# A hybrid two-layer encoder block on one core: conditioning loads and products moved ahead, a head's normalisation moved ahead of a weight split, four banks claimed at once

## The reference, cut to what matters

```
c_act = silu(c)
mod = c_act @ cond_w[layer] + cond_b[layer]          # (1, 6*1024): 12 pieces of 512 columns a layer
# layer 0: f = gated DeltaNet (4 heads, chunks of 64) beside window attention (8 heads), then SwiGLU
a_qkv, a_z, a_a, a_b, b_q, b_k, b_v = split_cols(h @ w_in, EVEN_WIDTHS)
# layer 1: f = retention, then top-2-of-8 expert SwiGLU
q, k, v, g = split_cols(h @ w_in, ODD_WIDTHS)        # 4 heads: q, k 256 wide, v, g 512 wide
y = multiscale_retention(rotary(q), rotary(k), v)    # per head
y = (y - mean(y)) * rsqrt(var(y) + eps) * gn_w       # the head's normalisation
out = (silu(g) * y) @ w_out
```

## Time and profile before

| | |
|---|---|
| median of 3 runs | 1683.41 us (1683.18 to 1684.49) |
| the profiled execution, its own time | 1683.41 us |
| its span in the profile | 1681.5 us |
| TensorE busy | 1602.5 us, 95% |
| VectorE busy | 1289.4 us, 77% |
| ScalarE busy | 1010.4 us, 60% |
| DMA, mean | 306 GB/s |

### The profile page before, as it was taken

The page is one execution under the profiler, slowest core; times in us unless marked ns, Lnnn a source line. Parts: engine busy times, 40 slices in busy tenths (PEclk is TensorE's granted clock), DMA queues, the critical chain, the costliest instruction groups (busy, mean ns, idle before and its releaser), DMA issues.

```text
span 1681.5 us, 20080 instructions
## 1 busy us (share of the span) xinstructions
PE 1602.5 (95%) x7810; PEld 1289.5 (77%) x7810; DVE 1289.4 (77%) x1176; ACT 1010.4 (60%) x868; POOL 104.3 (6%) x78
## 2 busy tenths in 40 slices
PE   3899999999989999699999999999999999999996
PEld 1785766888868888578888888888888888888875
DVE  1675657655577665889898898898898988988987
ACT  0452335444354553377777777777777777777775
POOL 0003110200001002010000000000000000000004
PEclk9999999999999999799999999999999999999998
DMA  9579596954545544499999999999999999999994
GB/s 327 198 279 336 209 366 213 299 188 167 211 135 175 191 152 139 164 350 396 376 388 377 377 389 372 385 389 369 384 389 370 388 383 373 389 385 362 389 377 151
DMA packets 234370, 515.33 MB, mean 306 GB/s; under 512 B 8936, under 2 KB 40960, under 8 KB 234176
## 3 DMA queue, kind: packets, MB, share of 16 engines
q1 hardware_dynamic: 228272, 491.99, 79.9%
q10 hardware_dynamic: 2992, 11.79, 2.0%
q0 software_dynamic: 3008, 10.20, 2.0%
HBM read 507.15 MB, written 13.11 MB: 309 GB/s over the span
## 4 chain that ended last, share of the span: by engine, by line
PE 91%; DVE 4%; DMA 2%; ACT 1%; issue 1%; POOL 0%; POOLq 0%; SPq 0%; DVEq 0%
PE bank L752 27%; PE bank L754 27%; PE bank L753 27%; PE bank L731 2%; PE bank L923 2%; DMA ring<-in_cond_w 2%; PE bank L1189 1%; PE bank L747 1%; PE bank L1101 1%; PE bank L1171 0%; DVE w_lo L1679 0%; PE bank L764 0%; PE bank L1180 0%; PE bank L984 0%; PE bank L1132 0%
## 5 line engine op out<-in xcount | busy, mean ns | idle before, releaser
L1679 DVE TENSOR_TENSOR w_lo<-ring,w_hi 128x2048 fp32r<-128x2048 f32 x336 | 764.7, 2290 | 104.3 <-ACT w_hi L1564 102.3
L1564 ACT ACTIVATE w_hi<-ring 128x2048 fp32r<-128x2048 f32 x334 | 640.5, 1918 | 195.2 <-PE bank L754 190.3
L752 PE MATMUL bank<-w_lo,heT_hi 128*128 128x512 f32 x896 | 353.9, 395 | 3.8 <-DVE w_lo L1679 2.2
L754 PE MATMUL bank<-w_hi,heT_hi 128*128 128x512 f32 x896 | 349.9, 391 | 0.0
L753 PE MATMUL bank<-w_hi,heT_lo 128*128 128x512 f32 x896 | 349.1, 390 | 0.0
L1668 DVE TENSOR_TENSOR w_part<-ring,w_part 128x1024 fp32r<-128x1024 f32 (+1 forms) x162 | 201.1, 1250 | 164.1 <-ACT w_part L1316 158.7
L1316 ACT ACTIVATE w_part<-ring 128x1024 fp32r<-128x1024 f32 (+1 forms) x162 | 169.2, 1049 | 234.1 <-PE bank L754 219.5
L752 PEld LDWEIGHTS bank<-w_lo,heT_hi 128*128 128x128 f32 x896 | 168.4, 188 | 39.0 <-issue 5.9
L754 PEld LDWEIGHTS bank<-w_hi,heT_hi 128*128 128x128 f32 x896 | 168.2, 188 | 35.7
L753 PEld LDWEIGHTS bank<-w_hi,heT_lo 128*128 128x128 f32 x896 | 168.5, 188 | 33.5
L752 PE MATMUL bank<-w_part,hT_hi 128*128 128x512 f32 (+1 forms) x448 | 178.8, 399 | 6.1 <-DVE hT_lo L1659 5.0
(11 more groups left out here) (345 smaller groups left out, 1532.4 us busy)
## 6 DMA issues: line engine op xcount, KB each, us to landing
ring<-in_moe_w_up SPq DMA_DIRECT2D x224, 1024.0 KB, 8.6
ring<-in_moe_w_down SPq DMA_DIRECT2D x112, 1024.0 KB, 7.3
ring<-in_cond_w SPq DMA_DIRECT2D x24, 2048.0 KB, 10.0
ring<-in_ffn_w_up SPq DMA_DIRECT2D x22, 1024.0 KB, 8.2
ring<-in_od_w_in SPq DMA_DIRECT2D x8, 2048.0 KB, 7.9
ring<-in_ev_w_in SPq DMA_DIRECT2D x5, 2048.0 KB, 10.1
ring<-in_ffn_w_down SPq DMA_DIRECT2D x5, 2048.0 KB, 7.5
ring<-in_od_w_in SPq DMA_DIRECT2D x8, 1024.0 KB, 7.7
```

The costliest lines, as they stand in the source:

```text
L752: mm(bank, lhs[0], rhs[1], start=start, stop=False)
L754: return mm(bank, lhs[0], rhs[0], start=False, stop=stop)
L1564: f(w_hi[:, n % 3], half_landed(act, it, u, half), ACT.Copy) \
L1679: tt(w_lo[:, buf], at, w_hi[:, buf].bitcast(F32), ALU.subtract).then_inc(S["w_lo"], 1)
```

## The change

Four edits in one.

The loads: a conditioning unit is put in front of `ev_in` 5, 4 and 3 each (two in front of 3), so that unit 5, 4 and 3 stand one, one and two places later than before (and from `cond(0, 10)` on the order is as it was). `COND_BATCHES` moves two units from its third batch to its second.

The rows: `cond_rows()` also runs after `ev_in` 2, and after `ev_in` 4 it takes two instead of one; after chunk 2 of the recurrence none is taken, and the last call takes one instead of two.

The banks: `down` claims its four banks ahead of its first part instead of each when it is first used.

The head's normalisation: ScalarE and VectorE no longer split part 3 of `od_v` ahead of `deviations` and `head_norm(h-1)`; the following `split_ahead("od_v", h)` does it after them.

```diff
-COND_BATCHES = (tuple((0, u) for u in FIRST_COND), tuple((0, u) for u in range(4, N_COND)) + tuple((1, u) for u in range(3)),
-                tuple((1, u) for u in range(3, N_COND)))
+COND_BATCHES = (tuple((0, u) for u in FIRST_COND), tuple((0, u) for u in range(4, N_COND)) + tuple((1, u) for u in range(5)),
+                tuple((1, u) for u in range(5, N_COND)))
...
-    order = c(0, *FIRST_COND) + e(0) + c(0, 4) + e(1) + c(0, 5) + e(2, 5) + c(0, 6) + e(4)
-    order += c(0, 7) + e(3) + c(0, 8, 9, 10, 11) + c(1, *range(N_COND))
+    order = c(0, *FIRST_COND) + e(0) + c(0, 4) + e(1) + c(0, 5) + e(2) + c(0, 6) + e(5) + c(0, 7)
+    order += e(4) + c(0, 8, 9) + e(3) + c(0, 10, 11) + c(1, *range(N_COND))
...
-                if u < 2:
-                    cond_rows()
+                cond_rows()
...
             project(("ev_in", 5), 0, 256)
             cond_rows()
             project(("ev_in", 4), 0, second=norms, second_at=(2, 0))
-            cond_rows()
+            cond_rows(2)
             project(("ev_in", 3), 0, second=norm_rows, second_at=(2, 0))
             cond_rows(2)
...
-                if n < 3:
+                if n < 2:
                     cond_rows()
...
-                outs = {}
+                outs = {(t, h): to_fill(pe, kind, t, h) for t in range(NT) for h in range(2)}
...
-                            if ch == 0:
-                                outs[t, h] = to_fill(pe, kind, t, h)
...
                 if h:
-                    split_to(part_no["od_v", h, 3] + 1)
                     deviations("ret_var", "ret_rstd", NT * (h - 1), eps_n)
                 split_ahead("od_v", h)
...
                 if h:
-                    split_to(part_no["od_v", h, 3] + 1)
                     head_norm(h - 1)
                 split_ahead("od_v", h)
```

## The result

The changed kernel takes 1699.40 us (median of 4 runs, 1696.13 to 1700.53) where the kernel before took 1683.73 us beside it (4 runs, 1683.18 to 1684.49). The ratio is 1.0101, with a 95% interval of 1.0086 to 1.0117: slower, by 15.7 us between the medians. The forecast was 1697.0. The profiled execution took 1700.71 us, 17.3 more than the one of before.

A forecast was written before the change was run, and what follows sets the result against it. TensorE, busy 95% of a 1681.5 us span, was taken as the bound. Terms 3.7 + 2.8 - 0.6 + 6.6 + 1.1 = 13.6 us on 1683.4 gave 1697.0 us, with an 8 in 10 range of 1690.5 to 1702.

The forecast's parts named there:

- term 2: At the first matmul of ev_in 4, TensorE waits 2.8 us because the unit's load lands late; ends 0 and 4.
- Term 1: Ahead of g_row, two more conditioning rows at 1.85 us each make it 3.7 us later; a cost of 3.7 us.
- prediction's own sign of being wrong: Wrong if g_row came within 2 us of its old time, od_v showed no wait, or the clock fell in new places.
- the rival's four falls: Each of four new TensorE waits is followed by half clock, 1.6 us lost each, 6.4 us added: 1703.4; chance 0.13.
- Term 3: In the recurrence's last chunk, a row less between kv and ws lets ws begin earlier; a gain of 0.6 us.
- Term 4: In od_v of heads 1 to 3, normalisation ahead of part 3's split makes TensorE wait; 2.2 us each, 6.6 us.
- The rival that had VectorE catch up: In od_v, VectorE catches up inside the stream and the 6.6 us cost fails to appear: 1690.4 us; chance 0.07.
- Term 5: At the start of od_out, claiming four banks at once holds TensorE for ScalarE's silu of head 3's tile 0; 1.1 us.

The follow-up runs named there:

- three part doses: Kernel before with only a part of the normalisation, a different part for each head, ahead of VectorE's split of od_v part 3; 1689.51 us (one run).
- VectorE run: Kernel before with the normalisation ahead of the split of od_v part 3 on VectorE alone, ScalarE's order unchanged; 1694.24 us (one run).
- two rows later: Kernel before with no conditioning row after ev_in 3, two ahead of xt and one between xt of tile 0 and tile 1; 1683.23 us (one run).

## Why the prediction was right, point by point

The forecast was 13.6 us over the profiled execution; that execution of the changed kernel came 17.3 us over it, and the medians 15.7. Each of the five terms was there, and for the reason given. But the landing in term 2 was mis-sized, and a fall of the clock was left out of the sum.

**Term 1, two more rows ahead of `g_row`: right**, and a little over-sized: 3.4 us for 3.7. Without the late unit A grew by 3.38 in all, and the two runs with it differ by 3.46, of which 0.09 are their waits; a row taken away gave 1.70 us, two gave 3.63. Why the price isn't always 1.85 us a row is open.

**Term 2, unit 4 lands late: right in kind, mis-sized.** Forecast 2.8, measured 4.20. The arrival of TensorE was forecast well: 104.86 and the 0.4 us that this execution started later make 105.3, and it came at 105.47. The issue too: 97.25 became 97.74. The landing was not. The answer for DMA issues from 97 to 98 us (KB, us to landing) has

```profile
ring<-in_ev_w_in SPq DMA_DIRECT2D x1, 2048.0 KB, 9.3
```

where I had taken 8.1 from one load. Loads of the same size in the trace of before, from 62 and from 174 us, have

```profile
ring<-in_cond_w SPq DMA_DIRECT2D x1, 2048.0 KB, 9.3
```

```profile
ring<-in_cond_w SPq DMA_DIRECT2D x1, 2048.0 KB, 9.2
```

so the spread could have been read beforehand. In the changed kernel a second load is issued at 100.72, beside this one. But `ev_in` 3's, issued at 117.60, when the load ahead of it had all but landed (117.71), and with none behind it until 129.54, took 9.3 us as well, so company alone is not the cause; what decides between 8 and 9.3 us stays open. One load was measured where a range was wanted; it costs 1.2 of the 1.4 us. In the four executions in which unit 4 is late its landing took from 8.8 to 9.3 us and the wait went with it, from 3.73 to 4.20.

**The clock: the sum left out 1.9 us, and the prediction's own sign of being wrong came true.** It was to be wrong if the granted clock had fallen in places where it had not, and at `ev_in` 4 it did. Behind the wait of 4.2 us the granted clock fell at once, and then again behind the one-column matmuls. In the changed kernel:

```profile
110.00:113.40 3.40, 3.40 (x10) 0.51 1.05 387
113.50:120.30 6.80, 6.80 (x48) 1.00 0.54 174
120.30:123.70 3.40, 3.40 (x10) 0.50 1.05 407
```

A of the changed kernel is 55.68 + 3.4 + 4.20 + 1.9, the last for the fall and the restart, as in the run with the late unit alone. Of the rival's four falls one came. In all, of 12 waits of 2.1 us in `od_v`, in four executions, one was followed by a fall, while all four waits of 3.7 to 4.2 us at `ev_in` 4 were. The Trainium skill (TensorE: Matmul & The Clock Gate, Part 1: The HAM clock gate) lets idleness bring the half rate back; these runs agree in 4 of 4 waits of about 4 us and in 1 of 12 of 2.1 us.

**Term 3, a row less in the recurrence: right.** `ws` waits 1.26 us where 1.2 was forecast. The profile names no releaser (`issue`), but VectorE's state ends at 238.27 and `ws` begins at 238.38. B is 0.55 us shorter in the run with rows and loads only than in the one with the late unit only, which keeps that row; forecast 0.6. Against the kernel before only 0.26 is seen, and the fall of the clock in B comes 1 us later after `g_row` in both, over other matmuls; that this makes the other 0.3 us is argued and not shown.

**Term 4, normalisation ahead of the split: right.** The waits are 3 x 2.09 us and the cost 3 x 2.33, forecast 3 x 2.2, and the three part doses confirm it. The place and the releaser were those named. The rival that had VectorE catch up is refuted.

**Term 5, four banks at once: right**, a wait of 1.17 us and a cost of 1.4, forecast 1.1. The forecast let TensorE begin 0.05 us after the silu's end; it was 0.34 (644.29 and 644.63). The releaser that I had said the profile would show (ScalarE's silu) is not the one that it names; the run with three banks showed that the reason was right and the name in the bracket was not.

The sum by what was measured: 3.4 + 4.2 + 1.9 - 0.3 + 7.2 = 16.4, and with 0.4 at the start and 0.6 in E 17.4, the growth of the span. The 7.2 are 8.4 for terms 4 and 5 less the 1.2 by which the start of D was shorter. By its terms the change cost this execution 17.6 us against the 13.6 forecast; that the medians came within 2.4 us of the forecast is in part luck.

## What to carry to other kernels

Before work is put ahead of something in an in-order queue, work out how long that something may be late (here 4.08 us less 1.22 for itself) and compare it with what is put ahead: up to that it cost nothing here, and beyond it each microsecond cost one, with some 0.25 us on top for each wait. For what arrives by a load, take both ends of the landings seen, not one of them. And ask of each new wait in a dense stretch whether the clock will fall behind it. An operation moved earlier gains nothing where the profile shows no wait for it, and loses its own length where the stretch is full; the gain lies in moving it the other way, out of the full stretch and into a wait, until the loads become late. Claim a resource when it is first used and not all at once, for the last claim can then hold back the first use.

## What the runs showed of the hardware that I had not expected

A wait that TensorE spends idle can cost more than its length: behind the 1.83 us of waiting that end at 156.29 before came 3.4 us at half speed, and when the wait was filled with a row, B became 1.3 us shorter beside the 1.7 us that A had gained. That the fall makes these 1.3 us fits the 1.5 us by which B grew in the VectorE run, where the fall at this place was 3.4 us longer. Not every such wait brings one: in the run with two rows later none follows the 1.83 us that end at 160.69.

The spread between executions of one kernel (1681.93 to 1688.49 us) may be made in good part in the start. That is argued from other kernels, for only one execution of the kernel before has a trace, and the two of the changed kernel began `ev_in` 2 within 0.03 us of each other. From 24 to 57 us TensorE's granted clock in two kernels that don't differ in that stretch was, in the run with rows and loads only and in the run with four banks (us, PE, PEclk, DMA share, GB/s):

```profile
24.00:57.00 33.00, 21.11 (x124) 0.84 0.83 304
```

```profile
24.00:57.00 33.00, 22.40 (x96) 0.70 0.83 304
```

and `ev_in` 2 began at 82.0 in the one and 86.3 us in the other. An edit worth 1 us can't be told from single runs here, while A repeats within 0.1 us (55.68 in the kernel before, and 55.65 to 55.69 in the five kernels that don't touch it) and C does too. D, with a spread of 1.4 us, and E, with 2.2, do not.
